# Routing weights of one dense token block by accumulating GpSimd transfers into the DRAM table

## The reference

```python
q = (hb @ w_q).reshape(n, 8, 2, 128)                     # 8 heads, 2 sides
s = einsum('nhid,hikd->nhik', q, sub_keys)               # 128 scores a side
s_top, i_top = top_k(s, 16)
cand = s_top[:, :, 0, :, None] + s_top[:, :, 1, None, :]
cand_idx = i_top[:, :, 0, :, None] * 128 + i_top[:, :, 1, None, :]
best, pos = top_k(cand.reshape(n, 8, 256), 16)
idx = take_along_axis(cand_idx..., pos)                  # 128 experts of 16384 a token
w = softmax(best)
act = gelu(einsum('nhkd,nd->nhk', u_tab[idx], hb))
out = einsum('nhk,nhkd->nd', w * act, v_tab[idx])
```

## Time and profile before

| | us |
|---|---|
| time, median of 3 executions | 2803.05 (2798.11 to 2810.21) |
| span of the profiled execution | 2796.3 |
| of it, up half of the PEER layer (956.6 to 1611.1) | 654.5 |
| of it, down half (1615.3 to about 2148) | 533 |
| TensorE busy | 2731.3 (98%) |
| VectorE busy | 1927.1 (69%) |
| GpSimd busy | 622.5 (22%) |

### The profile page before, as it was taken

One profiled execution on the slowest core, in us unless ns is written; L12 is line 12 of the kernel. 1 busy time (PEld: TensorE's weight loads), 2 busy tenths in 40 slices (PEclk: granted clock), 3 DMA queues, 4 the chain that ended last, 5 costly groups with the idle time before them and its releaser, 6 DMA issues. The chain is left out here.

```text
span 2796.3 us, 42880 instructions
## 1 busy us (share of the span) xinstructions
PE 2731.3 (98%) x15970; PEld 2449.9 (88%) x15970; DVE 1927.1 (69%) x3328; ACT 1030.0 (37%) x1502; POOL 622.5 (22%) x436
## 2 busy tenths in 40 slices
PE   8999999999999998999999999999999999999998
PEld 7887788898787898999999999999998877788887
DVE  7676563434545579999968778888888655588843
ACT  6433343223333343444444333333334333332222
POOL 4333100000000166566665322222221000100000
PEclk9999999999999999999999999999999999999999
DMA  3111222211222367899999999999996211233332
GB/s 131 46 54 55 75 96 78 75 45 60 95 94 99 95 186 265 253 292 287 301 285 354 360 322 339 338 339 338 339 337 238 68 54 61 68 98 98 98 89 78
DMA packets 254582, 488.29 MB, mean 175 GB/s; under 512 B 102737, under 2 KB 160209, under 8 KB 253666
## 3 DMA queue, kind: packets, MB, share of 16 engines
q1 hardware_dynamic: 199138, 326.88, 35.9%
q0 software_dynamic: 36864, 134.23, 13.2%
q10 hardware_dynamic: 18432, 25.17, 2.6%
HBM read 437.97 MB, written 48.23 MB: 174 GB/s over the span
## 5 line engine op out<-in xcount | busy, mean ns | idle before, releaser
L285 PE MATMUL banks<-experts_third,weights_high 128*128 128x384 f32 x1024 | 342.1, 334 | 1.1 <-DVE experts_third L2317 1.1
L287 PE MATMUL banks<-experts_third,weights_low 128*128 128x384 f32 x1024 | 342.0, 334 | 0.0
L286 PE MATMUL banks<-experts_third,weights_high 128*128 128x384 f32 x1024 | 342.0, 334 | 0.0
L2128 POOL TENSOR_TENSOR weights_low<-weights_raw,weights_high 128x1024 fp32r<-128x1024 f32 x66 | 158.3, 2398 | 473.7 <-ACT weights_high L2030 463.4
L2087 ACT ACTIVATE weights_high<-weights_raw 128x1024 fp32r<-128x1024 f32 x128 | 135.9, 1062 | 338.6 <-PE banks L287 338.6
L285 PE MATMUL banks<-hn_high,weights_high 128*128 128x264 f32 (+1 forms) x736 | 253.6, 345 | 4.2 <-DVEq L2677 1.7
L285 PE MATMUL banks<-hb_high,weights_high 128*128 128x384 f32 x688 | 238.7, 347 | 9.1 <-POOL weights_low L2128 9.1
L286 PE MATMUL banks<-hn_low,weights_high 128*128 128x264 f32 (+1 forms) x736 | 246.2, 335 | 0.0
L287 PE MATMUL banks<-hn_high,weights_low 128*128 128x264 f32 (+1 forms) x736 | 245.8, 334 | 0.0
L286 PE MATMUL banks<-hb_low,weights_high 128*128 128x384 f32 x688 | 232.0, 337 | 0.0
L287 PE MATMUL banks<-hb_high,weights_low 128*128 128x384 f32 x688 | 231.9, 337 | 0.0
(11 more groups left out here) (575 smaller groups left out, 7087.0 us busy)
## 6 DMA issues: line engine op xcount, KB each, us to landing
weights_raw<-in_u SPq DMA_DIRECT2D x128, 512.0 KB, 3.5
weights_raw<-in_v SPq DMA_DIRECT2D x128, 512.0 KB
early_experts<-experts_A ACTq DMA_DIRECT2D x128, 192.0 KB
shared<-early_experts SPq DMA_DIRECT2D x128, 192.0 KB
weights_raw<-in_w_up SPq DMA_DIRECT2D x44, 512.0 KB, 3.4
expert_weights<-shared SPq DMA_DIRECT2D x40, 512.0 KB
shared<-expert_weights SPq DMA_DIRECT2D x128, 160.0 KB
weights_raw<-in_w_xbc SPq DMA_DIRECT2D x24, 512.0 KB, 3.4
```

Of the source, the lines that this page charges most:

```text
L285: nc.tensor.matmul(to, w[0], x[0], start=start, stop=False)
L286: nc.tensor.matmul(to, w[0], x[1], start=False, stop=False)
L287: return nc.tensor.matmul(to, w[1], x[0], start=False, stop=stop)
L2128: nc.gpsimd.tensor_tensor(u_places[t % 3][1], raw[:, t % RING, :], u_places[t % 3][0].bitcast(F32), ALU.subtract).then_inc(u_low, 1)
```

## The change

Block 1 (tokens 128 to 255) no longer goes through `turn`, `one_hots`, `spread`, `copy_out` and `store_part`. Its columns of `w_dram`, 0 to 127 of the 320 stored, are set to zero in the queries phase by eight stores of 1 MB each, which SyncE issues behind the loads of `w_q`. After block 1's choice VectorE computes, for every token and (head, rank) pair, the place of its element in the table (`place`, as integers) and keeps the weight (`place_w`). GpSimd then issues 128 indirect transfers (`scatter`), each of which adds 128 elements of 4 bytes, one of each token, to the table. They stand between the low part and the gathers of a tile: one in every second tile from 31 to 55, three in each of the 20 tiles that hold one-hot products (56 to 60, 68 to 72, 83 to 87, 95 to 99), two or three in each tile from 100 to 124. Every sixteenth waits until all before it have landed, since two heads may choose the same expert. SyncE waits for all 128 before it loads table rows. The groups of blocks 2 and 3 keep their tiles; the exponential of block 2 moves from tile 50 to 46. `DOT_AT`, `GATHER_AT` and `SLOT_OF` are unchanged.

```diff
-EXP_AT = (13, 27, 50, 76)
-SPREAD_AT = [start + min(i // 3, 4) for start in (30, 42, 56, 68, 83, 95) for i in range(HALF // PER)]
+SCATTERED, SPREAD_BLOCKS = (1,), (2, 3)
+SPREAD_HALVES = [2 * (b - 1) + i for b in SPREAD_BLOCKS for i in range(2)]
+EXP_AT = (13, 27, 46, 76)
+SPREAD_AT = [start + min(i // 3, 4) for start in (56, 68, 83, 95) for i in range(HALF // PER)]
+SCATTER_READY = {1: 30}
+SCATTER_AT = [t for t in range(31, 125) for _ in range(
+    2 + (t % 4 == 0) if t > 99 else 3 if t in SPREAD_AT else t % 2 if t < 56 else 0)][:P * len(SCATTERED)]
+ZERO_PARTS = 8
...
@@ queries_phase
+        zeros = sb("zeros", [P, len(SCATTERED) * P])
...
             def _(sp):
+                sp.wait_ge(constants_set, 1)
                 for m in range(RING, TILES):
                     sp.wait_ge(low_done, m - RING + 1)
                     sp.dma_start(raw[:, m % RING, :], w_q[m]).then_inc(w_in[m % RING], 16)
+                    if m - RING < ZERO_PARTS:
+                        rows = KEYS // ZERO_PARTS
+                        sp.dma_start(w_dram[(m - RING) * rows:(m - RING + 1) * rows, :, 0:len(SCATTERED) * P].rearrange("i j n -> j i n"),
+                                     zeros[:].unsqueeze(1).to_broadcast([P, rows, len(SCATTERED) * P])).then_inc(zeroed, 16)
...
+                sp.wait_ge(zeroed, 16 * ZERO_PARTS)
...
+                nc.vector.memset(zeros[:], 0.0).then_inc(constants_set, 1)
...
@@ experts_phase
+        place, place_w = sb("place", [P, len(SCATTERED), P], U32), sb("place_w", [P, len(SCATTERED), P])
+        column = sb("column", [P, NB])
+        table = w_dram.rearrange("i j n -> (i j n)").unsqueeze(1)
...
-                sp.wait_ge(chosen_out, NB - 1)
-                sp.wait_ge(w_stored, 16 * STORES * (HALVES - 1))
+                sp.wait_ge(chosen_out, len(SPREAD_BLOCKS))
+                sp.wait_ge(w_stored, 16 * STORES * (len(SPREAD_HALVES) - 1))
+                sp.wait_ge(scattered, 16 * len(SCATTER_AT))
...
+                def scatter(n):
+
+                    b, g = n // P, n % P
+                    if g == 0:
+                        pool.wait_ge(row_index, 4 + 3 * (b + 1))
+                    elif g % TOPK == 0:
+                        pool.wait_ge(scattered, 16 * n)
+                    nc.gpsimd.indirect_dma_start(table, bass.IndirectOffsetOnAxis(ap=place[:, b, g:g + 1], axis=0),
+                                                 place_w[:, b, g:g + 1], None, compute_op=ALU.add).then_inc(scattered, 16)
+
                 for t in range(TILES):
...
                                                 ALU.subtract).then_inc(u_low, 1)
+                    for n in scatters_after(t):
+                        scatter(n)
                     for g in gathers_after(t):
...
                 for b in range(1, NB):
...
+                    if b in SCATTERED:
+                        i = SCATTERED.index(b)
+                        settle()
+                        step_f = row_f[:]
+                        nc.vector.scalar_tensor_tensor(step_f, picked[:, 0, :], float(KEYS), picked[:, 1, :], ALU.mult, ALU.add
+                                                       ).then_inc(row_index, 1)
+                        nc.vector.tensor_copy(place_w[:, i, :], picked[:, 2, :]).then_inc(row_index, 1)
+                        dve.wait_ge(row_index, 6 + 3 * i)
+                        nc.vector.tensor_scalar(place[:, i, :], step_f, float(STORED), column[:, i:i + 1], ALU.mult, ALU.add
+                                                ).then_inc(row_index, 1)
+                        route_scores(b + 1, sum(d < start + 12 for d in DOT_AT))
+                        continue
```

More of the change, by code:

```diff
@@ L1614, with queries_phase @@
 STORE_AFTER = (4, 5, 5, 6, 7, 7, 8, 9)
-def queries_phase(k, name, following, h, weight, w_q, pre, hb, q, normed, sq, total, turned):
+def queries_phase(k, name, following, h, weight, w_q, pre, hb, q, normed, sq, total, turned, w_dram):
     nc = k.nc
@@ L1790, in gathers_after, with scatters_after @@
     return [g for g in range(P) if GATHER_AT[g] == t]
+def scatters_after(t):
+    return [n for n in range(len(SCATTER_AT)) if SCATTER_AT[n] == t]
 def slot_uses(g):
@@ L1805, in block_begun @@
     groups = spread_groups(t)
-    return groups[0] // (HALF // PER * 2) + 1 if groups and groups[0] % (HALF // PER * 2) == 0 else 0
+    return SPREAD_BLOCKS[groups[0] // (HALF // PER * 2)] if groups and groups[0] % (HALF // PER * 2) == 0 else 0
 def experts_phase(k, name, following, q, out, keys, hb, u, v, u_rows, by_token, gathered, early, w_dram, ws, es, keys_loaded):
@@ L1886, in store_part @@
                         sp.wait_ge(copied, (half + 1) * GROUPS)
+                    to = SPREAD_HALVES[half] * HALF
                     r = slice(part * KEYS_PART, (part + 1) * KEYS_PART)
-                    sp.dma_start(w_dram[r, :, half * HALF:(half + 1) * HALF].rearrange("i j n -> j i n"), out[:, r, :]
+                    sp.dma_start(w_dram[r, :, to:to + HALF].rearrange("i j n -> j i n"), out[:, r, :]
                                  ).then_inc(w_stored, 16)
@@ L1893, in _ @@
                         sp.dma_start(raw[:, t % RING, :], u[t]).then_inc(raw_in[t % RING], 16)
-                    for half in range(HALVES - 1):
+                    for half in range(len(SPREAD_HALVES) - 1):
                         last = SPREAD_AT[(half + 1) * GROUPS - 1]
@@ L2256, in one_hots @@
                         dve.wait_ge(spread_done, n - 1)
-                    four = slice(n * PER, (n + 1) * PER)
-                    here = (n * PER) % P
+                    four = slice(column_of(n), column_of(n) + PER)
+                    here = column_of(n) % P
                     pairs = [P, 2, PER, P]
@@ L2273, in _ @@
                 nc.vector.tensor_copy(row_i[:], row_f[:]).then_inc(row_index, 1)
+                nc.vector.tensor_tensor_reduce(below, k.const("ident"), k.const("iota"), 1.0, 0.0, ALU.mult, ALU.add, column[:, 0:1]
+                                               ).then_inc(row_index, 1)
+                dve.wait_ge(row_index, 4)
                 for b in range(1, NB):
-                    start = SPREAD_AT[(b - 1) * 2 * GROUPS]
+                    spread_from = SPREAD_BLOCKS.index(b) * 2 * GROUPS if b in SPREAD_BLOCKS else 0
+                    start = SPREAD_AT[spread_from] if b in SPREAD_BLOCKS else SCATTER_READY[b]
                     dots_to = sum(at < start for at in DOT_AT)
@@ L2281, in _ @@
                         dot()
-                    dve.wait_ge(chosen_out, b)
-                    for n in range((b - 1) * 2 * GROUPS, b * 2 * GROUPS):
+                    if b in SCATTERED:
[7 more added lines that the diff above has]
+                        nc.vector.tensor_scalar(place[:, i, :], step_f, float(STORED), column[:, i:i + 1], ALU.mult, ALU.add
+                                                ).then_inc(row_index, 1)
+                        route_scores(b + 1, sum(d < start + 12 for d in DOT_AT))
+                        continue
+                    dve.wait_ge(chosen_out, SPREAD_BLOCKS.index(b) + 1)
+                    for n in range(spread_from, spread_from + 2 * GROUPS):
                         at = SPREAD_AT[n]
-                        if n == (2 * b - 1) * GROUPS and b + 1 < NB:
+                        if n == spread_from + GROUPS and b + 1 < NB:
                             route_scores(b + 1, sum(d < at for d in DOT_AT))
```

41 lines of the change are left out of this document (21 added, 20 removed).

## The result

The changed kernel takes 2913.97 us (median of 4 runs, 2913.03 to 2919.25) against 2806.63 us (median of 4, 2798.11 to 2810.63): ratio 1.0407, 95% interval 1.0388 to 1.0426. I had forecast 2821 us and a range up to 2876. The sign was right, the size was not: some 110 us more instead of 18. How much more depends on what is compared. The medians differ by 107 us (3.8%), the ratio of 4.1% stands for 114 us, and the two profiled spans, 2911.2 and 2796.3 us, differ by 114.9 us. The execution profiled after took 2913.03 us, 1.8 us over its span. Differences between the experiments are taken from their ratios, and a ratio of 0.01 is 28 us.

The account below looks back on a forecast made before the run. TensorE's instruction count was taken as the bound, GpSimd next. The terms -31.1 + 11 + 14.1 + 4.2 + 19.3 = +17.5 us on a 2796.3 us span gave 2814, carried to 2821 us by 6.8; range 2775 to 2876.

Parts of the forecast that it names:

- The sign: Whole kernel: slower, by 18 us; chances 0.55 slower, 0.24 same, 0.21 faster.
- What bounds the kernel: Up and down halves: the count of TensorE's instructions bounds, and GpSimd is the next that it waits for.
- The removal: 32 one-hot groups, block 1's transposes and a wait leave TensorE's path: 31.1 us less.
- the 11 us: Tiles 31 to 55: GpSimd full, waiting for dot products; 5 us lost at tiles 34 to 36, 6 at 44 to 47.
- The zero stores at nothing: Queries phase: eight zero stores between loads of w_q fit in their tiles and cost 0.
- The scatter priced as a gather: GpSimd: an accumulating transfer takes a gather's 0.985 us, 1.285 with the gap, 164 us for 128; chance 0.52.
- The slope of the sum: Overloaded blocks, tile 95 on and early burst: 118 us more for each us of a scatter's period.
- rival 2: The accumulating write is dear: at 1.97 us an instruction 116 us more, 2937 us, or slow landings, 2876; chance 0.18.
- The end as one queue: From tile 95 on GpSimd has no gap left; last gather issued at 1627.8 us, 19.3 us lost at the turn.
- The blocks: Tiles 56, 68 and 83 on, five each: GpSimd overloaded, 4.7 us lost in each, 14.1 in all.
- the landings at scatters 32 and 48: GpSimd waits for the scatter just before to land: 2.1 us twice, 4.2 us.
- Gathers of u and of v: Gathers of v in the down half take 1.071 us, of u 0.985: same 4 KB rows, beside other work on VectorE.

Follow-up runs that it names:

- run 2: The changed kernel with its 128 transfers writing instead of accumulating (one of two weights lost where two heads choose the same expert): 2851.0 us, ratio 1.0191.
- Runs 11 and 12: VectorE's dot products from tile 103 on two tiles later in its program, in the changed kernel with writing (2842.47 us) and with accumulating scatters (2908.71 us).
- run 1: The changed kernel without its 128 accumulating transfers (block 1's weights missing from the table): 2774.69 us, ratio 0.9913.
- run 4: The changed kernel with all 128 transfers, each for 64 of the 128 tokens: 2892.69 us, ratio 1.0329.
- run 7: The changed kernel, its scatters spread over tiles 31 to 124, VectorE making the low parts of tiles 51 to 55 and 88 to 94: 2855.33 us, ratio 1.0190.
- run 3: The changed kernel with every other scatter left out, 64 issued: 2798.21 us, ratio 1.0003.

## Why the prediction was wrong, step by step

**What bounds the kernel: right.** TensorE first, GpSimd next; the loss stands where GpSimd makes the low parts and gathers.

**The removal: right.** I had -31.1 + 11 = -20 us for the early tiles; the changed kernel gains 20.5 us there. The run without scatters gains 21.7 us, so what was lost of the 31.1 was not the scatters'. Its slow tiles are 35 and 36 (8.6 and 6.5 us instead of 4.2) and 45 and 46 (7.1 and 6.5), 12 us together at the two places that I had named for the 11 us. At the first GpSimd waited for a dot product of VectorE before a gather, and so came late with the low part:

```profile
1135.69 0.96 POOL L2137 DMA_INDIRECT shared<-in_u_rows,experts_row_i  x1 [5.26 <-DVE experts_dots L2191]
```

The windows of this run at the two places, PE first, the clock behind POOL:

```profile
1137.00:1145.00 8.00, 5.93 (x21) 5.93 (x22) 7.85 (x8) 0.00 (x0) 6.66 (x3) 0.57 0.64 203
1145.00:1153.00 8.00, 8.00 (x48) 8.00 (x47) 7.83 (x50) 3.12 (x4) 4.31 (x3) 1.00 0.41 140
...
1185.00:1193.00 8.00, 4.94 (x27) 4.62 (x28) 7.10 (x14) 4.49 (x6) 5.58 (x5) 1.00 0.80 256
```

**The zero stores at nothing: right.** From 867 to 960 us TensorE is busy for 92.09 of 93 us with them and 92.68 without, though the DMA share went from 0.29 to 0.62. That is 0.6 us at the most.

**The scatter priced as a gather: the step that failed, by size.** "I take the gather, 0.985 us, the same form over the same 128 rows." It is 1.607 us in the mean, within the bounds of 0.33 and 1.97, in the upper half. The form was priced rightly (0.99 us as a write); the accumulation is what no row of before held. The slope of the sum, 118 us for each us of the period, would make 118 x (1.607 - 1.037) = 67 us of the difference of the means; 60 us were measured. So the sum was sensitive in about the right measure, and rival 2, which I gave 0.18, is what happened, at 0.6 of what it added to the instruction.

**The end as one queue: wrong in kind.** I followed GpSimd to its last gather and put the end of its dot product 4.7 us behind its start, 19.3 us after the old turn. Near my own price (run 2, 1.037 us in the mean) the stretch from tile 95 to the gelu is 42.1 us longer than without scatters. The slack between the last gather and the gelu, 29.5 us before (1612.21 - 1582.72), did not shrink to 5 but to 20.3: that is 15.6 us of the miss. Another 5.5 us are GpSimd's own, whose last gather starts 175.9 us after tile 95 and not 170.4. From tile 100 on VectorE makes the low part of each tile behind dot products that wait for rows; so a late gather holds the tile, and TensorE doesn't run ahead of GpSimd. Runs 11 and 12 bear this out: the order loosened by two tiles gives 5.6 and 4.2 us of this stretch back. That the order makes all of the 15.6 us is not shown. Missed: 22.8 us.

**The blocks: right in kind, too small.** 4.7 us in each and 2.1 us for the landings at scatters 32 and 48: 18.3 us. In run 2 the stretch from tile 30 to 95 loses 34.1 us against run 1: 4.6, 13.0 and 7.6 us in the blocks, 8.9 us in the tiles between. The first block is met to 0.1 us. In the second GpSimd waited 3.9 us for the landing and 4.5 us for a high part of ScalarE, and I had let it start each block with its full lead of 5.1 us. Which of these made the rest was not tried apart. Missed: 15.8 us.

The sum with the misses: 17.5 + 58.2 (price, from the traces) + 22.8 + 15.8 - 5.2 (the removal is 25.3 us from tile 0 to the gelu in run 1, not 20.1) = 109.1 us, which is by construction what lies between tile 0 and the gelu. The spans differ by 114.9: 4.4 us more lie ahead of tile 0 and 1.4 behind the gelu. Tile 0 of the profiled executions varies by as much (958.9 to 965.1 us over all of them, with and without scatters). The 0.052 us by which run 2's mean lies over my 0.985 would be 6 us by the slope of the sum, and are contained in the last two misses. The sign was not luck: at about my own price, in run 2, the kernel is slower too.

**Gathers of u and of v.** Gathers of u beside the scatters took 1006 and 981 ns, 996 and 963 before; the scatters lie close together (1551 ns at the least, 1577 in the median; five of them are 0.3 to 1.0 us longer, and the mean is 1607). The gathers of v, 1.071 us before, don't show that other work on VectorE made them dearer: gathers of u and of v differ in table, buffers and stage too. The 0.6 us comes and goes with the accumulation alone (1037 ns in the mean without it, run 2). In run 4 an address counts for little, 2.4 ns, but the estimated 1.27 us that stay are far from small on an engine that is full. What they consist of no run shows.

**A version that beats both** was not found. The best with all 128 accumulating scatters is run 7, 2855 us, and half of them (run 3) already cost what the removal brings.

## What to carry to other kernels

Before work is moved to an engine that isn't the bound, add up that engine's time by stretch, gaps between instructions included, and look at who stands behind it: here 240 us went into some 180 us of free time, with the makers of the next tile's operands in the same queue. An operation that the profile doesn't hold is not priced by its nearest form: one run with the accumulation and one without would have shown 1.58 against 0.99 us. And where two engines' programs are woven tile by tile, the order of the program can limit how far one may run ahead of the other: here two tiles of looser order brought 5.6 and 4.2 us, and of 21 us taken from GpSimd ahead of its last gather 18.7 came back in TensorE's up half.

## What the runs showed of the hardware beyond this

**TensorE's clock fell in the gaps.** With the same 15,711 matmuls TensorE is busy for 2749.2 us in the changed kernel and for 2707.5 us without scatters. Windows of 4 us of the changed kernel, columns as above:

```profile
1624.00:1628.00 4.00, 1.78 (x11) 1.46 (x9) 0.30 (x2) 1.55 (x2) 3.08 (x4) 1.00 0.71 134
1628.00:1632.00 4.00, 0.00 (x0) 0.00 (x0) 1.23 (x2) 0.00 (x0) 3.39 (x3) 0.52 1.00 377
1632.00:1636.00 4.00, 1.44 (x4) 1.44 (x5) 3.86 (x6) 0.00 (x0) 3.09 (x4) 0.50 0.59 133
1636.00:1640.00 4.00, 4.00 (x18) 4.00 (x18) 2.01 (x3) 0.00 (x0) 3.70 (x2) 0.70 0.94 321
1640.00:1644.00 4.00, 4.00 (x25) 4.00 (x24) 2.37 (x3) 1.56 (x2) 3.08 (x4) 1.00 0.76 177
```

The gap behind them, on TensorE's timeline:

```profile
1634.56 0.69 PE L285 MATMUL banks<-hb_high,experts_third 128*128 128x384 f32 x1 [8.78 <-DVE experts_third L2349]
```

TensorE stood still for 8.8 us, until 1634.56, and the granted clock went to 0.50. After it worked again the clock was 0.70 in the window from 1636 and 1.00 in that from 1640. I had expected no such thing, since before the clock was 1.00 from 1100 to 1600 us and 0.98 from 957 to 1100 us, where it was at 0.50 in the window from 1092, around a wait of TensorE of 5.88 us. How much of the 42 us is a loss of its own stays open: where GpSimd was full, as from 1607.8 to 1677 us, a faster TensorE may only have waited longer.

**The price of an accumulating indirect transfer on GpSimd** (128 addresses, 4 bytes each, into DRAM): 1.58 us, 1.43 us for 64 addresses, 0.99 us without the accumulation, and 0.30 us of gap before each. Its landing held GpSimd only four times, 9.4 us in all.
